# Second block of a two-block model: the mix product split into a pooled half and a convolution half, with the convolution's norm placed beside the pooled half

## What is computed

```
p = h @ w_in                                  # 1024 -> 5 * 1024
a_val, a_glu, a_gate, b_val, b_gate = split(p)
u = a_val * sigmoid(a_glu)
u = causal_depthwise_conv(u, conv_w, conv_b)  # 31 taps
u = silu(layernorm(u, ln_g, ln_b))
ya = u * silu(a_gate)
d = multiscale_pool_diff(b_val)               # windows 2, 4, 8, 16; minus b_val
d = einsum(d, pool_w) + pool_b                # 4 groups of 256 x 256
yb = d * pool_scale * silu(b_gate)
y = concatenate([ya, yb]) @ w_out             # 2048 -> 1024, added to x
```

## Time and profile before

| | us |
|---|---|
| median of 3 runs | 1905.85 (1903.43 to 1906.97) |
| the profiled execution, its time | 1908.41 |
| its span in the trace | 1906.6 |
| TensorE matmul busy | 1765.6 (93% of the span) |
| VectorE busy | 854.0 (45%) |
| ScalarE busy | 661.6 (35%) |
| GpSimd busy | 849.9 (45%) |
| mean share of the full TensorE clock granted | 0.963 |

### The profile page before, as it was taken

The page is one execution under the profiler, slowest core; times in us unless marked ns, Lnnn a source line. Parts: engine busy times, 40 slices in busy tenths (PEclk is TensorE's granted clock), DMA queues, the critical chain, the costliest instruction groups (busy, mean ns, idle before and its releaser), DMA issues.

```text
span 1906.6 us, 22668 instructions
## 1 busy us (share of the span) xinstructions
PE 1765.6 (93%) x9095; PEld 1476.9 (77%) x9095; DVE 854.0 (45%) x1344; ACT 661.6 (35%) x965; POOL 849.9 (45%) x464
## 2 busy tenths in 40 slices
PE   4989978999999999999999999989777989999987
PEld 4879878898988888877888878868555768877766
DVE  4457954833423301122111220169999671157732
...
DMA packets 119840, 201.39 MB, mean 106 GB/s; under 512 B 32144, under 2 KB 71208, under 8 KB 119736
## 3 DMA queue, kind: packets, MB, share of 16 engines
...
...
## 4 chain that ended last, share of the span: by engine, by line
PE 70%; DVE 18%; ACT 3%; issue 3%; DMA 3%; POOL 2%; SPq 1%; DVEq 0%; ACTq 0%
PE ps L393 56%; DVE ps L1185 7%; PE ps L1671 3%; DVE cacc L2032 2%; PE ps L844 1%; DMA w_raw<-in_w 1%; DVE tmp L2224 1%; POOL w_lo L381 1%; PE ps L890 1%; PE ps L854 1%; PE ps L897 1%; DMA d_p<-dec 1%; PE ps L852 1%; PE ps L901 1%; DVE inv L584 1%
## 5 line engine op out<-in xcount | busy, mean ns | idle before, releaser
L381 POOL TENSOR_TENSOR w_lo<-w_raw,w_hi 128x1024 fp32r<-128x1024 f32 x264 | 633.5, 2409 | 635.0 <-ACT w_hi L375 635.0
L393 PE MATMUL ps<-hp_hi,w_hi 128*128 128x512 f32 (+2 forms) x1760 | 589.1, 365 | 41.5 <-DVE u_in L2208 13.7
L393 PE MATMUL ps<-hp_lo,w_hi 128*128 128x512 f32 (+2 forms) x1760 | 580.6, 360 | 0.0
L393 PE MATMUL ps<-hp_hi,w_lo 128*128 128x512 f32 (+2 forms) x1760 | 579.4, 359 | 0.0
L393 PEld LDWEIGHTS ps<-hp_hi,w_hi 128*128 128x128 f32 x1760 | 316.8, 193 | 105.0 <-issue 22.4
L393 PEld LDWEIGHTS ps<-hp_lo,w_hi 128*128 128x128 f32 x1760 | 317.1, 193 | 51.4 <-issue 2.2
L393 PEld LDWEIGHTS ps<-hp_hi,w_lo 128*128 128x128 f32 x1760 | 316.2, 192 | 49.5
L375 ACT ACTIVATE w_hi<-w_raw 128x1024 fp32r<-128x1024 f32 x264 | 277.3, 1053 | 184.9 <-DMA w_raw<-in_w 161.4
L1185 DVE SCALAR_TENSOR_TENSOR ps<-u_in,par,ps 128x511 f32<-128x511 f32 (+14 forms) x240 | 177.4, 739 | 8.0
L2032 DVE SCALAR_TENSOR_TENSOR cacc<-ps,par,cacc 128x528 f32<-128x528 f32 x96 | 73.6, 767 | 65.6 <-ACT cacc L1711 63.0
L393 PE MATMUL ps<-mx_hi,w_hi 128*128 128x512 f32 x144 | 59.9, 416 | 18.0 <-ACT tmp L1893 7.3
...
## 6 DMA issues: line engine op xcount, KB each, us to landing
w_raw<-in_w SPq DMA_DIRECT2D x264, 512.0 KB, 3.4
...
d_y<-zero SPq DMA_DIRECT2D x1, 4128.0 KB, 27.9
...
```

The source lines that it names most:

```text
L381: e.tensor_tensor(w_lo[:, u % RAW, :], w_raw[:, u % RAW, :], w_hi[:, u % RAW, :].bitcast(F32), ALU.subtract).then_inc(s_lo, 1)
L393: mm = e.matmul(ov, w, r[:, k, t0:t1], start=(first and n == 0 and p3 == 0), stop=(last and n == len(tiles) - 1 and p3 == 2))
```

## The change

The diff touches the unit table, the order on all engines from *glu* to *mix*, and the place of a few intermediate results.

- The first two glu units are taken together. All 32 products that need only the rounded activations stand first, those with the remainders last.
- Convolution steps are 31 for each tile. The copy to `uc` is done by ScalarE (`act_uc`), at a fixed place in its program, and the third tile and those after it start only when the copy of the tile two before is done. The 248 steps are dealt out as 13 behind each glu tile, BV_STEPS behind the bval tiles, 28, then 5 ahead of each pooled product's scaling, 28, and BG_STEPS ahead of the bgate tiles' products.
- Four agate units stand ahead of *pool*, four behind it. Each bval, pool, agate and bgate unit waits for its own bank alone.
- The silu of bgate is written back to its PSUM bank, and VectorE multiplies from there.
- *mix* becomes *mixb* (8 units on the pooled half) and then *mixa* (8 units on the convolution's half), each with an addition to `x` of its own.
- The layer norm moves from *bgate* to *mixb*. Its squares are summed as 32 products with one column each, root and reciprocal are taken of four columns, and the factors are broadcast by `pe_spread`. TensorE waits for the reciprocal in line, between the third and the fourth unit of *mixb*. The silu goes to PSUM banks 6 and 7.

The core of the diff (from the glu units on, only what is new and what stays; what is taken out stands in the functions printed above):

```diff
-         ("out", KT), ("gu", 2 * FT), ("down", 3 * KT), ("glu", 2 * KT), ("bval", KT), ("pool", 4),
-         ("agate", KT), ("bgate", KT), ("mix", 2 * KT), *((f"{n}{g}", m) for g in range(LT // 3) for n, m in (("xr", 3), ("lgate", 3), ("lru", 1))),
+         ("out", KT), ("gu", 2 * FT), ("down", 3 * KT), ("glu", 2 * KT), ("bval", KT), ("agate0", 4), ("pool", 4),
+         ("agate1", 4), ("bgate", KT), ("mixb", KT), ("mixa", KT), *((f"{n}{g}", m) for g in range(LT // 3) for n, m in (("xr", 3), ("lgate", 3), ("lru", 1))),
...
+BV_STEPS = [4, 4, 3, 3, 3, 2, 2, 1]
+BG_STEPS = [6, 6, 6, 6, 6, 6, 5, 5]
...
         def conv_steps(e, first, n):
 
             for i in range(first, first + n):
-                k, t = divmod(i, TAPS + 1)
-                if t:
+                k, t = divmod(i, TAPS)
+                acc, w = ps[:, 6 + k % 2, :], pcol("ca", k, TAPS - 1 - t)
+                if t == 0:
+                    e.wait_ge(*dv.at("glu", k + 1))
+                    if k > 1:
+                        e.wait_ge(*au.at("c", k - 1))
+                    e.tensor_scalar(acc, u_in[:, k, :], w, pcol("cab", k), ALU.mult, ALU.add).then_inc(cl.sem, 1)
+                else:
                     e.wait_ge(*cl.at("c", i))
-                elif k > 1:
-                    e.wait_ge(*cl.at("c", (k - 1) * (TAPS + 1)))
-                conv_step(e, k, t).then_inc(cl.sem, 1)
+                    e.scalar_tensor_tensor(acc[:, t:SEQ], u_in[:, k, 0:SEQ - t], w, acc[:, t:SEQ], ALU.mult, ALU.add).then_inc(cl.sem, 1)
+
+        def act_uc(e, k):
+            e.wait_ge(*cl.at("c", TAPS * (k + 1)))
+            e.activation(uc[:, k, :], ps[:, 6 + k % 2, :], ACT.Copy).then_inc(au.sem, 1)
 
...
+            u = BASE["glu"]
+            e.wait_ge(s_lo, u + 2)
+            for lo_part in (False, True):
+                for k in range(KT):
+                    e.wait_ge(*(lo if lo_part else hi).at("n3", k + 1))
+                    for i in range(2):
+                        wh, wl = (w[:, (u + i) % RAW, k * P:(k + 1) * P] for w in (w_hi, w_lo))
+                        if lo_part:
+                            mm = e.matmul(ps[:, i, :], wh, h_lo[:, k, META:T1], start=False, stop=k == KT - 1)
+                            if k == KT - 1:
+                                mm.then_inc(s_pe, 1)
+                        else:
+                            e.matmul(ps[:, i, :], wh, h_hi[:, k, META:T1], start=k == 0, stop=False)
+                            e.matmul(ps[:, i, :], wl, h_hi[:, k, META:T1], start=False, stop=False)
+            for j in range(1, KT):
                 if j >= 2:
                     e.wait_ge(*dv.at("glu", j - 1))
...
+                gemm(e, u + 2 * j, [ps[:, 2 * (j % 2), :]], TOK, h_hi, h_lo, K8).then_inc(s_pe, 1)
                 if j >= 2:
                     e.wait_ge(*ev.at("glu", j - 1))
...
+                gemm(e, u + 2 * j + 1, [ps[:, 2 * (j % 2) + 1, :]], TOK, h_hi, h_lo, K8).then_inc(s_pe, 1)
+
             for j in range(KT):
...
+                e.wait_ge(*(ev.at("bval", j - 3) if j >= 4 else ev.at("glu", 7 + j // 2) if j % 2 else dv.at("glu", 7 + j // 2)))
                 gemm(e, BASE["bval"] + j, [ps[:, j % 4, :]], TOK, h_hi, h_lo, K8).then_inc(s_pe, 1)
...
             for j in range(4):
...
+                e.wait_ge(*ev.at("bval", j + 5))
+                gemm(e, BASE["agate0"] + j, [ps[:, j, :]], TOK, h_hi, h_lo, K8).then_inc(s_pe, 1)
+                sum_mu(e, j)
+            for j in range(4):
+                e.wait_ge(*(dv.at("pool", 2 * (j - 1)) if j >= 2 else ev.at("agate", 2 * j + 2)))
                 for o in range(2):
                     mm = gemm(e, BASE["pool"] + j, [ps[:, 2 * (j % 2) + o, :]], ALL, mx_hi, mx_lo,
                               [(2 * o + k, KT + 2 * j + k) for k in range(2)], ready=lambda k: lo.at("bval", k - KT + 1))
                 mm.then_inc(s_pe, 1)
...
+            for j in range(4):
+                e.wait_ge(*dv.at("pool", j + 5))
+                gemm(e, BASE["agate1"] + j, [ps[:, j, :]], TOK, h_hi, h_lo, K8).then_inc(s_pe, 1)
+                if j == 1:
+                    sum_mu(e, 4)
             for j in range(KT):
...
+                e.wait_ge(*(dv.at("bgate", j - 3) if j >= 4 else ev.at("agate", j + 5)))
+                gemm(e, BASE["bgate"] + j, [ps[:, j % 4, :]], TOK, h_hi, h_lo, K8).then_inc(s_pe, 1)
+                if j in (1, 6):
+                    sum_mu(e, 5 + j // 4)
+
             for j in range(KT):
...
+                e.wait_ge(*(dv.at("mixb", j - 3) if j >= 4 else dv.at("bgate", j + 5)))
+                gemm(e, BASE["mixb"] + j, [ps[:, j % 4, :]], ALL, mx_hi, mx_lo, [(t, KT + t) for t in range(KT)],
+                     ready=(lambda k: lo.at("bgate", k - KT + 1)) if j == 0 else None).then_inc(s_pe, 1)
                 if j == 0:
                     sum_mu(e, 7)
                 if j == 2:
                     for k in range(KT):
                         e.wait_ge(*sq.at("va", k + 1))
...
+                        for c in range(NCH):
+                            mm = e.matmul(ps[:, 5, c:c + 1], row(k)[:, c * P:(c + 1) * P], cmat("mean1024")[:, 0:1],
+                                          start=k == 0 and c == 0, stop=k == KT - 1 and c == NCH - 1)
+                    mm.then_inc(ss.sem, 1)
+                    e.wait_ge(*rc.at("va", 1))
+                    pe_spread(e, 5, 16).then_inc(tb_.sem, 1)
+
             for j in range(KT):
...
+                e.wait_ge(*(dv.at("mix", j - 3) if j >= 4 else dv.at("mixb", j + 5)))
+                gemm(e, BASE["mixa"] + j, [ps[:, j % 4, :]], ALL, mx_hi, mx_lo, K8,
+                     ready=(lambda k: lo.at("a", k + 1)) if j == 0 else None).then_inc(s_pe, 1)
 
 
...
+            round_unit(e, BASE["mixb"] + 2)
+            act_uc(e, 7)
+            round_unit(e, BASE["mixb"] + 3)
             e.wait_ge(*lo.at("bgate", KT))
...
+            for k in range(KT):
+                e.wait_ge(*ln.at("c", k + 1))
+                e.activation(row(k), uc[:, k, :], ACT.Square).then_inc(sq.sem, 1)
+            round_unit(e, BASE["mixb"] + 4)
+            e.wait_ge(*ss.at("va", 1))
+            e.activation(small[:, 16:20], ps[:, 5, 0:4], ACT.Sqrt, bias=eps5_col).then_inc(rt.sem, 1)
+            round_unit(e, BASE["mixb"] + 5)
+            for k in range(KT + 1):
+                if k < KT:
+                    e.wait_ge(*ln.at("n", k + 1))
+                    if k >= 2:
+                        e.wait_ge(*la.at("a", k - 1))
+                    e.activation(ps[:, 6 + k % 2, :], uc[:, k, :], ACT.Silu, bias=pcol("lnb", k), scale=pcol("lng", k)).then_inc(au.sem, 1)
+                if k >= 1:
+                    e.wait_ge(*la.at("a", k))
+                    e.activation(mx_hi[:, k - 1, :], row(k - 1), ACT.Copy).then_inc(hi.sem, 1)
+                if k in (2, 5):
+                    round_unit(e, BASE["mixb"] + 6 + k // 3)
+            round_unit(e, BASE["mixb"] + 8)
+            round_unit(e, BASE["mixb"] + 9)
...
+                conv_steps(e, n0, BV_STEPS[j])
+                n0 += BV_STEPS[j]
...
+            conv_steps(e, n0, 28)
+            n0 += 28
             for j in range(4):
+                conv_steps(e, n0, 5)
+                n0 += 5
                 e.wait_ge(s_pe, BASE["pool"] + j + 1)
                 for o in range(2):
                     e.tensor_scalar(yb[:, 2 * j + o, :], ps[:, 2 * (j % 2) + o, :], pcol("pb", 2 * j + o), pcol("psc", 2 * j + o), ALU.add, ALU.mult).then_inc(dv.sem, 1)
...
+            conv_steps(e, n0, 28)
+            n0 += 28
 
             for j in range(KT):
...
+                conv_steps(e, n0, BG_STEPS[j])
+                n0 += BG_STEPS[j]
                 e.wait_ge(*ev.at("bgate", j + 1))
+                e.wait_ge(*dv.at("pool", j + 1))
                 if j >= 2:
                     e.wait_ge(*lo.at("bgate", j - 1))
...
+                e.tensor_tensor(row(2 + j % 2), ps[:, j % 4, :], yb[:, j, :], ALU.mult).then_inc(dv.sem, 1)
+
+            def add_b(j):
+                e.wait_ge(s_pe, BASE["mixb"] + j + 1)
+                e.tensor_tensor(x[:, j, :], x[:, j, :], ps[:, j % 4, :], ALU.add).then_inc(dv.sem, 1)
+
+            e.wait_ge(*ss.at("mu", KT))
+            for k in range(KT):
+                e.tensor_tensor(uc[:, k, :], uc[:, k, :], ps[:, 4, :], ALU.subtract).then_inc(ln.sem, 1)
+            for j in range(3):
+                add_b(j)
+            e.wait_ge(*rt.at("va", 1))
+            e.reciprocal(small[:, 16:20], small[:, 16:20]).then_inc(rc.sem, 1)
+            e.wait_ge(*tb_.at("va", 1))
+            e.wait_ge(*ln.at("c", KT))
+            for k in range(KT + 1):
+                if k < KT:
+                    e.tensor_tensor(uc[:, k, :], uc[:, k, :], ps[:, 5, :], ALU.mult).then_inc(ln.sem, 1)
+                if k >= 1:
+                    e.wait_ge(*au.at("u", k))
+                    e.tensor_tensor(row(k - 1), ps[:, 6 + (k - 1) % 2, :], sg_a[:, k - 1, :], ALU.mult).then_inc(la.sem, 1)
+                if k == 4:
+                    add_b(3)
```

(3 more changed lines are left out.)

184 lines of the change are left out of this document (67 added, 117 removed).

## The result

The changed kernel takes **1871.99 us** (median of 4 runs, 1870.30 to 1873.56) against 1906.41 for the kernel before (1903.43 to 1909.62): a ratio of 0.9818, 95% interval 0.9802 to 0.9834. That is 34.4 us less, where 42.2 were forecast; the predicted 1863.6 is 8.4 us too low and the range of 1851 to 1882 holds the time. The profiled span is 1870.5 us.

What follows compares the result with a forecast made beforehand. VectorE was taken to bound the mixer up to the pooled products, TensorE behind them. 52.0 less 5.8 (clock) less 4.0 (VectorE against GpSimd) gave 42.2 us off 1905.85, so 1863.6; range 1851 to 1882.

Steps and rivals of the forecast that it cites:

- The bound: Mixer: VectorE leads up to the pooled products, then TensorE, which idles 8.6 us for the pool scaling.
- the signs named: Mixer trace: among others, no TensorE wait over 1 us elsewhere before mixb, and its last mix product near 1613.
- First glu units: Start of the mixer: products needing only the rounded tile go first, ending at 1267.0, a gain of 3.1 us.
- glu: Glu stage: TensorE leads to 1345.1, VectorE's last product comes at 1345.8, and the 13.7 us wait goes.
- bval, the step that failed: VectorE's window adds beside GpSimd: +4 us of stretching, bounds -4.3 and +23; first scaling at 1424.0 without it.
- The adds meet GpSimd each time: Rival in bval: VectorE stays the bound, 12 to 20 us more before agate1, say 1879; chance 0.18.
- The +8: VectorE's adds in bval: by the exclusive lock they could get worse as GpSimd is denser, towards +8.
- agate1, bgate and the convolution: Behind the pooled products: TensorE through at 1504.9, VectorE at 1503.9, arriving together with nothing lost.
- The clock in the column products: Norm in mixb: clock falls 4 us in; columns 2.3, broadcast 1.0, slow wide start 2.5, together 5.8 us.
- The rival of a clock that holds: Column products in mixb: the clock stays full through them, 48 us less, 1857.8; chance 0.22.
- Little won: Rival: conv steps spread but TensorE has gaps elsewhere, in mixa or mixb; gain 20, 1886; chance 0.06.
- slower: Rival: clock falls in the column products and stays low to the end of mixa, 1934; chance 0.03.

Runs made afterwards that it cites:

- e8: Changed kernel with the first two glu units run one after the other again, as in the kernel before: 1874.93 us.
- e12: Changed kernel with 6 conv steps behind each tile of pooled values and 2 instead of 28 ahead of the scalings: 1859.60 us.
- e2: Changed kernel with VectorE's first window add and last subtraction in bval taking one operand from PSUM instead of SBUF: 1866.62 us.
- e7: Changed kernel with PSUM operands in bval, columns inside mixb unit 3, spread behind unit 4, mean products moved, 14 conv steps put behind the last bgate product: 1849.36 us.
- e11: Changed kernel with the column products behind mixb unit 2 issued twice: 1884.87 us, median of two runs.

## Why the prediction was right, and where it was off

- **The bound** (VectorE up to the pooled products, TensorE behind) was read rightly: TensorE's long wait stands where it was put, and those said to go are gone. Two of the signs named were missed by a little: two waits for weight remainders ahead of mixb last 1.1 us, and TensorE's last mix product ends near 1618.7, not 1613.
- **First glu units:** 3.1 us forecast, 25.3 - 22.8 = 2.5 in the trace, 2.9 by e8.
- **glu:** VectorE's last product came at 1345.1 us, forecast 1345.8, with no wait behind it. In this profile all of the mixer lies 1.5 us earlier (sums at 1243.38 and not 1244.84), so counted from the sums it is 0.8 us late.
- **bval, the step that failed.** "I take +4, near the row itself, since the busy share rises by less than half." The adds took 28.6 - 17.9 = 10.7 us more. The first scaling started at 1433.8 and not 1424.0, which put agate1 at 1445.1 instead of 1435.3. I scaled the stretching by GpSimd's busy share. What decides is at which moment of GpSimd's program VectorE's add falls, and the change, by taking steps out from between the tiles, had moved the adds to an earlier moment of it: e12 does the same work with no stretching at all. So most of what the 16 steps fewer were to save in bval (16 x 0.77 = 12.3 us) was waited out beside GpSimd. The mechanism had been named ("The adds meet GpSimd each time"), as a rival that costs 12 to 20 us more than the forecast. By mechanism this rival came true, but at 6.7 us more than the 4 of the forecast, just over half of its least price; the 10.7 is within the bounds of -4.3 and +23.
- **Rule and trace.** By the Trainium skill, *SBUF — State Buffer*, "Who interferes with whom", VectorE with two SBUF inputs and GpSimd take turns under an exclusive lock. This case agrees: in e2 the adds with one PSUM operand take 684 ns, and adds that start 0.7 and 1.8 us into a weight (changed kernel, before) both end 0.55 us behind it. The +8 that I worked out by it was nearer to the 10.7 than my own 4.
- **agate1, bgate and the convolution** end together, as forecast, only later: VectorE's last bgate product starts at 1515.7. e7 shows that its order was not the best: 14 steps moved behind that product cost 0.8 us there, a wait for a square, and save the long one.
- **The clock in the column products** was read rightly, and its size came out exact by luck: 5.8 forecast; 9.97 - 6.3 = 3.7, 2.08 - 0.89 = 1.2 and 0.9 for the slow start make 5.8. The start had been put too high (2.5) and the columns too low (2.3), and the two errors cancel. It fell 3.7 us into them, 4 had been taken. The rival of a clock that holds fell with it, and so did the one that it stays low through mixa: e11 keeps it low for 20 us of columns, and it is back about 1.5 us into the wide products.
- **mixb and mixa:** the norm had cover, mixa waited for nothing, 44.65 us for eight units.
- **The sum:** 52.0 - 5.8 - 10.7 - 0.6 = 34.9 us, for 34.4 measured (the last term is the first glu units, 2.5 for 3.1).
- **Little won** and **slower** stay rivals that did not happen. Only two parts of the change were taken back by themselves, the first glu units (2.9 us) and the place of the pooled products (5.7). That the rest of the gain belongs to the waits that are gone is read from the traces, and how much of it is due to the split of the mix product alone stays open.
